# Two order changes in a two-layer fp32 kernel: what ScalarE and VectorE do around the first pair of each seven-product block, and a stacked layout for the long-convolution filters

## The reference, cut to what matters

```python
def swiglu_ffn(x, wi, wo):                  # d_model 1024, D_FF 2816, 512 tokens
    gate, up = jnp.split(x @ wi, 2, axis=-1)
    return (jax.nn.silu(gate) * up) @ wo

def hyena_filters(seqlen, w1, b1, w2, b2, w3, sin_freq):
    ...
    h = jnp.sin(sin_freq[0] * (zpos @ w1 + b1))
    h = jnp.sin(sin_freq[1] * (h @ w2 + b2))
    h = (h @ w3).astype(f32).reshape(seqlen, HY_ORDER, 2, HY_WIDTH)   # 512, 2, 2, 1024
    h = h * jnp.exp(-t * deltas)[:, None, None, :]
    return jnp.moveaxis(h, 0, 2)

def long_conv_bidir(u, h_fwd, h_bwd, bias):
    k = jnp.concatenate([h_fwd, jnp.zeros_like(h_fwd[:1]), h_bwd[:0:-1]], axis=0)
    ...                                     # product of spectra, inverse transform
```

## Time and profile before

| | |
|---|---|
| median of 3 runs | 4611.59 us (4609.36 to 4623.51) |
| profiled execution | 4627.68 us, its span 4625.9 us |
| PE busy | 4425.9 us (96%) |
| DVE busy | 3177.0 us (69%) |
| ACT busy | 1751.0 us (38%) |
| POOL busy | 2051.1 us (44%) |
| lines 2647 to 2649 (the seven products) on PE | 646.8 + 638.0 + 637.9 us |

### The profile page before, as it was taken

The page is one execution under the profiler, slowest core; times in us unless marked ns, Lnnn a source line. Parts: engine busy times, 40 slices in busy tenths (PEclk is TensorE's granted clock), DMA queues, the critical chain, the costliest instruction groups (busy, mean ns, idle before and its releaser), DMA issues.

```text
span 4625.9 us, 64527 instructions
## 1 busy us (share of the span) xinstructions
PE 4425.9 (96%) x25239; PEld 3828.8 (83%) x25239; DVE 3177.0 (69%) x4507; ACT 1751.0 (38%) x2753; POOL 2051.1 (44%) x1297
## 2 busy tenths in 40 slices
PE   7999999999999999999999999999999999998998
PEld 4757855779989999999899876798799878887997
DVE  4756667569869988788688355687488355555883
ACT  3334211233335543333345255444344243123442
POOL 2042024205887657788576100474276101124751
PEclk9999999999999999999999999899999999898999
DMA  4142411225776789999632321233232322001332
GB/s 174 52 145 96 145 62 54 91 87 172 258 240 218 256 330 391 375 384 385 235 96 92 100 75 46 73 101 96 78 99 94 96 85 73 24 33 59 97 101 73
DMA packets 229014, 664.15 MB, mean 144 GB/s; under 512 B 22039, under 2 KB 87975, under 8 KB 226536
## 3 DMA queue, kind: packets, MB, share of 16 engines
q1 hardware_dynamic: 112832, 398.26, 25.9%
q0 software_dynamic: 38752, 143.03, 8.4%
q10 hardware_dynamic: 77128, 118.73, 7.1%
HBM read 591.78 MB, written 68.16 MB: 143 GB/s over the span
## 4 chain that ended last, share of the span: by engine, by line
PE 63%; DVE 19%; POOL 7%; issue 5%; DMA 3%; ACT 3%; ACTq 0%; POOLq 0%; SPq 0%; DVEq 0%
PE ps L258 14%; PE ps L260 14%; PE ps L259 14%; DVE r L277 6%; POOL A L2882 3%; PE ps L1537 2%; DVE r L227 2%; POOL A L2823 2%; DVE A L1966 2%; PE ps L1616 1%; ACT r L274 1%; DVE A L2265 1%; PE ps L585 1%; DMA A<-in_f2i 1%; DMA A<-in_w_mod 1%
## 5 line engine op out<-in xcount | busy, mean ns | idle before, releaser
L258 PE MATMUL ps<-r,r 128*128 128x384 f32 (+2 forms) x3880 | 1427.2, 368 | 19.5 <-POOL r L227 11.6
L260 PE MATMUL ps<-r,r 128*128 128x384 f32 (+2 forms) x3880 | 1410.4, 363 | 0.0
L259 PE MATMUL ps<-r,r 128*128 128x384 f32 (+2 forms) x3880 | 1410.3, 363 | 0.0
L227 DVE TENSOR_TENSOR r<-A,r 128x1024 fp32r<-128x1024 f32 x428 | 585.5, 1368 | 718.0 <-ACT r L221 717.4
L221 ACT ACTIVATE r<-A 128x1024 fp32r<-128x1024 f32 x505 | 534.5, 1059 | 1246.4 <-PE ps L260 1046.9
L258 PEld LDWEIGHTS ps<-r,r 128*128 128x128 f32 x3880 | 733.2, 189 | 110.4 <-issue 20.4
L259 PEld LDWEIGHTS ps<-r,r 128*128 128x128 f32 x3880 | 732.9, 189 | 78.8 <-issue 3.4
L260 PEld LDWEIGHTS ps<-r,r 128*128 128x128 f32 x3880 | 732.2, 189 | 78.1
L277 DVE TENSOR_TENSOR r<-A,r 128x512 fp32r<-128x512 f32 x645 | 676.5, 1072 | 126.4 <-ACT r L274 122.6
L274 ACT ACTIVATE r<-A 128x512 fp32r<-128x512 f32 (+1 forms) x824 | 467.2, 607 | 712.3 <-POOL A L2882 431.8
L2647 PE MATMUL ps<-r,r 128*128 128x256 f32 x2240 | 646.8, 289 | 48.5 <-ACT A L2740 24.3
(11 more groups left out here) (526 smaller groups left out, 5839.4 us busy)
## 6 DMA issues: line engine op xcount, KB each, us to landing
A<-in_pu SPq DMA_DIRECT2D x128, 512.0 KB, 4.3
A<-in_pv SPq DMA_DIRECT2D x128, 512.0 KB, 6.8
A<-in_f1i SPq DMA_DIRECT2D x88, 512.0 KB, 3.5
A<-in_f2i SPq DMA_DIRECT2D x88, 512.0 KB, 3.5
A<-in_w_mod SPq DMA_DIRECT2D x48, 512.0 KB, 4.4
A<-in_w_in SPq DMA_DIRECT2D x48, 512.0 KB, 3.6
acts<-A ACTq DMA_DIRECT2D x128, 192.0 KB, 4.3
gates<-A ACTq DMA_DIRECT2D x8, 3072.0 KB, 11.4
```

Of the source, the lines that this page charges most:

```text
L227: e.tensor_tensor(self.vr(at + 1024, 1024), self.v(self.st0 + 1024 * (u % RS), 1024), self.vr(at, 1024).bitcast(F32), ALU.subtract).then_i ...
L258: t.matmul(o, hi, xh, start=first and k == k0, stop=False)
L259: t.matmul(o, hi, xl, start=False, stop=False)
L260: m = t.matmul(o, lo, xh, start=False, stop=final and k == K - 1)
```

## The change

Two things are changed.

In the blocks, the lists of ScalarE and VectorE are written in another order up to the start of pair 1. ScalarE now copies "one" of pair 0 directly behind the high part of operand 5, and makes the tokens' "22" high part and operands 6 to 10 behind it. VectorE makes the difference "22" only after operands 3, 4, 5 and `times_up` 1, and the table `EARLY_V` says which low parts stand behind which quarter sum for the first nine products. From the ninth product on both lists are as before.

In the filters, the second perceptron layer is made twice, on partitions 0 to 63 and 64 to 127 (its weights are loaded twice, side by side). The two 64-row weight slices are loaded to both partition halves too, the sum is made on the lower half and the difference on the upper half, and the two filters' products read different halves. The decay at tap 0 is halved on the host, and tap 0 is the sum of the two filters' first rows, copied to both, so the ninth product is gone.

```diff
@@ -1302,14 +1302,14 @@
         L.TB, L.KW, L.M, L.H2 = self.al(8192), self.al(2048), self.al(1536), self.al(512)
         L.DEC, L.W3 = self.HX, self.HX + 2048
         L.ZP, L.W12 = L.KW, L.KW + 1536
-        L.h, L.kk = self.A[0:64, L.KW + 1024:L.KW + 1536], self.A[0:64, L.KW + 512:L.KW + 1024]
-        L.hs = [self.A[0:64, L.H2:L.H2 + 512], self.A[0:64, L.W3 + 1536:L.W3 + 2048]]
-        L.a, L.b, L.sm = (self.A[0:64, L.W3 + 512 * i:L.W3 + 512 * i + 512] for i in range(3))
+        L.h, L.kk = self.v(L.KW + 1024, 512), self.v(L.KW + 512, 512)
+        L.hs = [self.v(L.H2, 512), self.v(L.W3 + 1536, 512)]
+        L.a, L.b, L.sm = (self.v(L.W3 + 512 * i, 512) for i in range(3))
 
         L.KWS, L.SQ = (L.OS, L.KW), L.OS + 2048
         L.ST = self.al(64)
 
-        fil, ks, us = (lambda r: [("fil", r, i) for i in range(9)]), (lambda r, f: [("ks", r, f, i) for i in range(4)]), (lambda r, f: [("us", r, f, i) for i in range(4)])
+        fil, ks, us = (lambda r: [("fil", r, i) for i in range(8)]), (lambda r, f: [("ks", r, f, i) for i in range(4)]), (lambda r, f: [("us", r, f, i) for i in range(4)])
         inv, tok = (lambda r: [("inv", r, c) for c in range(4)]), (lambda o: [("ut", o + i) for i in range(4)])
         self.plan([x for r in range(4) for x in us(r, 0) + us(r, 1) + inv(r)], range(4))
         self.plan([x for r in range(4) for x in fil(r) + (tok(4 * (r - 2)) if r in (2, 3) else []) + ks(r, 0) + ks(r, 1)], range(4, 8))
@@ -1320,8 +1320,8 @@
         L.parts = [(L.HF + 512 * k, L.TB + 512 * k) for k in range(8)]
         L.parts += [(L.UT + 512 * k, (L.OS if k < 4 else L.YF) + 512 * k) for k in range(8)]
 
-    def p64(self, name, k=0):
-        return self.A[0:64, self.prm0 + PRM[name][0] + k:self.prm0 + PRM[name][0] + k + 1]
+    def layer_rows(self, i):
+        return slice(0, 64) if i == 0 else slice(0, 128)
 
 
 
...
@@ -1332,16 +1332,17 @@
     def mlp_t(self, t, i):
         S, L = self.S, self.L2
         t.wait_ge(*S.at("hz") if i == 0 else S.at("layer", 0))
-        w, r = ((self.A[0:33, L.W12:L.W12 + 64], self.A[0:33, L.ZP:L.ZP + 512]), (self.A[0:64, L.W12 + 64:L.W12 + 128], L.h))[i]
-        t.matmul(self.PS[6][0:64, :], w, r, start=True, stop=True).then_inc(*S.on("t", "layer mm", i))
+        w, r = ((self.A[0:33, L.W12:L.W12 + 64], self.A[0:33, L.ZP:L.ZP + 512]), (self.A[0:64, L.W12 + 64:L.W12 + 192], L.h[0:64, :]))[i]
+        t.matmul(self.PS[6][self.layer_rows(i), :], w, r, start=True, stop=True).then_inc(*S.on("t", "layer mm", i))
 
     def mlp_v(self, v, i):
         S, L = self.S, self.L2
-        h, kk = L.h, L.kk
+        rows = self.layer_rows(i)
+        h, kk = L.h[rows, :], L.kk[rows, :]
         v.wait_ge(*S.at("layer mm", i))
-        v.tensor_scalar(h, self.PS[6][0:64, :], self.p64("hy_b1" if i == 0 else "hy_b2"), None, ALU.add).then_inc(*S.on("v"))
+        v.tensor_scalar(h, self.PS[6][rows, :], self.prm("hy_b1" if i == 0 else "hy_b2")[rows, :], None, ALU.add).then_inc(*S.on("v"))
         v.wait_ge(*S.last("v"))
-        v.tensor_scalar(h, h, self.p64("sinf", i), None, ALU.mult).then_inc(*S.on("v"))
+        v.tensor_scalar(h, h, self.prm("sinf", i)[rows, :], None, ALU.mult).then_inc(*S.on("v"))
         v.wait_ge(*S.last("v"))
         v.tensor_scalar(kk, h, float(1 / (2 * np.pi)), 12582912.0, ALU.mult, ALU.add).then_inc(*S.on("v"))
         v.wait_ge(*S.last("v"))
...
@@ -1461,7 +1462,8 @@
             a.wait_ge(*S.at("filter", r - 1))
         for i, x in enumerate((L.a, L.b)):
             at = 2048 * order + 1024 * i + 512 * half
-            a.dma_start(x, T["hy_w3"][:, at:at + 512]).then_inc(*S.dma("w3"))
+            for rows in (slice(0, 64), slice(64, 128)):
+                a.dma_start(x[rows, :], T["hy_w3"][:, at:at + 512]).then_inc(*S.dma("w3"))
         S.mark("w3", "w3", r)
         a.dma_start(self.v(L.DEC, 2048).rearrange("p (n c) -> p n c", n=4),
                     T["decay"][order].rearrange("(n p) c -> p n c", p=128)[:, :, 512 * half:512 * half + 512]).then_inc(*S.dma("dec", "filter decay", r))
@@ -1485,18 +1487,16 @@
             t.wait_ge(*S.at("u tokens", 0, 7))
             t.wait_ge(*S.at("hidden", 1))
         for nt in range(4):
-            for j, w in enumerate((L.sm, L.b)):
+            for j, rows in enumerate((slice(0, 64), slice(64, 128))):
                 ps = self.bank_t(t, "fil", r, 2 * nt + j)
-                t.matmul(ps[:, :], self.A[0:64, hh + 128 * nt:hh + 128 * nt + 128], w, start=True, stop=True).then_inc(*S.on("t", "fil", r, 2 * nt + j))
-        ps = self.bank_t(t, "fil", r, 8)
-        t.matmul(ps[0:1, :], self.A[0:64, hh:hh + 1], L.a, start=True, stop=True).then_inc(*S.on("t", "fil", r, 8))
+                t.matmul(ps[:, :], self.v(hh + 128 * nt, 128)[rows, :], L.sm[rows, :], start=True, stop=True).then_inc(*S.on("t", "fil", r, 2 * nt + j))
 
     def sums_v(self, v, r):
         S, L = self.S, self.L2
         v.wait_ge(*S.at("w3", r))
-        v.tensor_tensor(L.sm, L.a, L.b, ALU.add).then_inc(*S.on("v"))
-        v.wait_ge(*S.last("v"))
-        v.tensor_tensor(L.b, L.a, L.b, ALU.subtract).then_inc(*S.on("v", "filter sums", r))
+        for rows, how in ((slice(0, 64), ALU.add), (slice(64, 128), ALU.subtract)):
+            v.tensor_tensor(L.sm[rows, :], L.a[rows, :], L.b[rows, :], how).then_inc(*S.on("v"))
+        S.mark("v", "filter sums", r)
 
     def filters_v(self, v, r, ids):
         S, L = self.S, self.L2
@@ -1504,16 +1504,16 @@
         if r:
             v.wait_ge(*S.at("ks", r - 1, 1, 3))
         for i in ids:
-            v.wait_ge(*S.at("fil", r, i))
             nt, j = divmod(i, 2)
             if i < 8:
+                v.wait_ge(*S.at("fil", r, i))
                 v.tensor_tensor(self.v(L.HF + 2048 * j + 512 * nt, 512), self.ps("fil", r, i)[:, :], self.v(L.DEC + 512 * nt, 512), ALU.mult).then_inc(*S.on("v", "out", "fil", r, i))
                 continue
+            one, two = (self.A[0:1, L.HF + 2048 * j:L.HF + 2048 * j + 512] for j in range(2))
             v.wait_ge(*S.last("v"))
-            for j in range(2):
-                v.tensor_tensor(self.A[0:1, L.HF + 2048 * j:L.HF + 2048 * j + 512], self.ps("fil", r, 8)[0:1, :], self.A[0:1, L.DEC:L.DEC + 512], ALU.mult).then_inc(*S.on("v"))
-            S.mark("v", "out", "fil", r, 8)
-            S.mark("v", "filter", r)
+            v.tensor_tensor(one, one, two, ALU.add).then_inc(*S.on("v"))
+            v.wait_ge(*S.last("v"))
+            v.tensor_copy(two, one).then_inc(*S.on("v", "filter", r))
 
 
 
@@ -2710,6 +2710,7 @@
             a.wait_ge(*S.at("product", i, self.PAIRS - 1, {5: "s2", 9: "s1", 13: "s3", 17: "22"}[f]))
         self.part_hi(a, self.v(L.HID + 512 * f, 512), L.HI[f], 512, "hidden hi", i, f)
 
+    EARLY_V = {0: (), 1: (6,), 2: (7,), 3: (8,), 4: (9, 10), 5: (11, 12), 6: (13, 14), 7: (15, 16), 8: (17, 18)}
     LATE_A = {129: (0, 1), 130: (2, 3), 131: (4,), 134: (5,), 135: (6, 7), 136: (8, 9), 137: (10, 11), 138: (12,), 139: (13, 14)}
     LATE_V = {130: (0,), 131: (1,), 133: (3,), 134: (4,), 135: (6,), 136: (7,), 137: (9,), 138: (10,)}
 
@@ -2727,10 +2728,7 @@
                 self.token_a(a, i, "s3")
                 for n in range(1, 3):
                     self.operand_a(a, i, n)
-        for n in range(3, 7):
-            self.operand_a(a, i, n)
-        self.token_a(a, i, "22")
-        for n in range(7, 11):
+        for n in range(3, 6):
             self.operand_a(a, i, n)
         for m, (p, x) in enumerate(L.seven):
             if x == "11":
@@ -2740,6 +2738,10 @@
                 a.activation(self.v(L.CU + 512 * (p % 2), 256), self.ps("A", i, p)[:, 0:256], ACT.Copy).then_inc(*S.on("a", "one", i, p))
                 if p:
                     self.gate_half_a(a, i, p - 1, 1)
+                else:
+                    self.token_a(a, i, "22")
+                    for n in range(6, 11):
+                        self.operand_a(a, i, n)
             if x == "12":
                 self.gate_half_a(a, i, p, 0)
             self.operand_a(a, i, m + 11)
@@ -2839,18 +2841,18 @@
         self.operand_v(v, i, 1)
         self.token_lo_v(v, i, "s1")
         self.operand_v(v, i, 2)
-        self.token_v(v, i, "22")
         self.operand_v(v, i, 3)
         self.token_lo_v(v, i, "s3")
+        for n in range(4, 6):
+            self.operand_v(v, i, n)
         self.times_up_v(v, i, 1)
-        for n in range(4, 7):
-            self.operand_v(v, i, n)
-        self.token_lo_v(v, i, "22")
-        for n in range(7, 10):
-            self.operand_v(v, i, n)
+        self.token_v(v, i, "22")
         for m, (p, x) in enumerate(L.seven):
             self.quarter_v(v, i, p, x)
-            self.operand_v(v, i, m + 10)
+            if m == 1:
+                self.token_lo_v(v, i, "22")
+            for n in self.EARLY_V.get(m, (m + 10,)):
+                self.operand_v(v, i, n)
             for f in self.LATE_V.get(m, ()):
                 self.hidden_lo(v, "v", i, f)
             if m == 132:
@@ -4399,6 +4401,7 @@
```

(1 more changed line is left out.)

9 lines of the change are left out of this document (5 added, 4 removed).

## The result

| | before | after |
|---|---|---|
| median, 20 runs each on one chip | 4623.52 us | 4613.43 us |
| lowest and highest | 4609.36 to 4630.58 | 4604.66 to 4627.15 |
| ratio of the changed kernel to the one before | | 0.9982, 95% interval 0.9974 to 0.9991 |
| profiled execution | 4627.68 us | 4606.66 us |

By the ratio the change makes the kernel 8.3 us faster (4 to 12); the two medians lie 10.1 us apart. With 20 runs each, 8.3 us is told from none.

The account below looks back on a forecast made before the run. A loop of VectorE, GpSimd and ScalarE was taken to set the blocks' period, with TensorE waiting in it. Blocks 1.6 and filters 4.6 us off 4611.59 gave a median of 4605, range 4588 to 4616.

Parts of the forecast that it names:

- the filters' term: Filter rounds: overlap and the missing ninth product gain 2.2 + 1.4 + 1.0 = 4.6 us (3 to 7).
- The blocks' term: Four blocks: the new order of the lists gains 0.4 us a block, 1.6 in all.
- the limit of 0.3%: Whole kernel: a change of 0.3% (14 us) is about what this measurement tells from none.
- The stall moves, not goes.: Blocks: TensorE's 5.99 us wait at product 3 goes, and some 4.3 us of waiting appears at product 10.
- Operand 7 isn't earlier.: Blocks, VectorE: operand 7's low part stays 11.7 us behind product 0, within 0.7, so the raw load doesn't move.
- `gated` of pair 0 at 22.3, 0.5 us earlier.: Blocks: `gated` of pair 0 starts about 22.3 us behind product 0 (22.9 before), with the period of a pair unchanged.
- the first rival: Blocks: the 5.99 us wait and half clock go with nothing in their place, 4 times 10 us, 4565; chance 0.16.
- The clock at product 10: Blocks: after 4.3 us of idleness TensorE may run at 1.2 GHz from product 10, losing 4 us.
- The slower rival: Blocks: product 10 at half clock makes product 14 late, 10.4 us a launch lost, 4617 with the filters; chance 0.11.
- its sum of 5.9: Filters: the gain of about 5.9 us if the two row halves overlap as the skill states, without it 3.3.
- 4595 (VectorE faster up to operand 7): Blocks: the new order keeps GpSimd off the port, 2.9 us a block, 16 with the filters; chance 0.14.
- "Nothing": Filters and blocks: neither gives anything, 4609 to 4612; chance 0.07.

Follow-up runs that it names:

- e2: The kernel before with only the new order of the blocks' lists, filters as they were; ratio 1.0006 to before.
- e5: The changed kernel with four extra matmuls of constants on TensorE ahead of product 10 of each block; ratio 0.9981 to before.
- e4: The kernel before with ScalarE's order alone changed: "one" of pair 0, then the tokens' high part "22", directly behind operand 6; ratio 1.0006 to before.
- e8: The changed kernel with operand 7 made early, and "one" of pair 1 and the SiLU half ahead of operands 15 and 16; ratio 0.9976 to before.
- e7: The changed kernel with operand 7's high and low parts made ahead of the token difference "22"; ratio 0.9984 to before.
- e6: The changed kernel with ScalarE's "one" of pair 1 and SiLU half of pair 0 ahead of operands 15 and 16; ratio 1.0007 to before.
- e9: e6 with VectorE's quarter sums "one six" and "one five" of pair 1 ahead of the low parts of operands 15 to 18; ratio 0.9976 to before.
- e11: The changed kernel with only VectorE's quarter sums of pair 1 moved ahead of the low parts of operands 15 to 18; ratio 1.0004 to before.
- e10: e8 with VectorE's quarter sums of pair 1 ahead of the low parts of operands 15 to 18; ratio 0.9983 to before.
- e3: The kernel before with only the ninth filter product gone (halved decay at tap 0), filters not stacked on two halves; ratio 0.9986 to before.

## Why the prediction was right or wrong

The step that failed is the filters' term. It was put at 4.6 us and measured 8.2: the overlap of the two halves was counted half where it is full, VectorE's fourth copy-out of round 1 was held to stay where it was, and two transposes were moved ahead of the wait where four more go. The blocks' term was too large (1.6 against 0.9 or none). The mechanism of both terms is what the traces show; that 6.2 lies so near the measured 8.3 is in part luck, since the two errors pull in opposite directions. The second thing that failed is the limit of 0.3% below which a change was held not to be told from none: the interval of the ratio is 4 us to each side.

- **The stall moves, not goes.** Right. Product 10 was to start 22.1 us behind product 0 (35.35 against 13.28) and starts at 22.12; the idleness was put at 4.3 and is 4.18.
- **Operand 7 isn't earlier.** Right: forecast to end at 11.7 us behind product 0, it ends at 11.9. GpSimd's first sum again goes ahead only at VectorE's operation on PSUM: the sum starts at 1.15 us and takes 3.92, `times_up` starts at 3.84, and the VectorE operations that began in between, at 1.50, 2.64 and 3.24 us, kept their usual lengths (1.21, 0.67 and 0.68). That is the reading of the earlier trace rows and again not the order that the Trainium skill ("SBUF — State Buffer", "Who interferes with whom") gives; the price of that order, 0.8 us lost a block, didn't come.
- **`gated` of pair 0 at 22.3, 0.5 us earlier.** Nearly: 22.54 to 22.63, 0.2 to 0.5 us earlier than in the profile of before (mean 0.3). Blocks of other kernels with the old order reach 22.56 too, so even this isn't clear of scatter. The first period is 10.55 to 10.59 us (10.60 to 10.63 before), unchanged for this purpose.
- **0.4 us a block, 1.6 in all.** Measured 0.9 in the changed kernel and none in e2, which has the same lists. So a gain of the blocks is not shown; that it is far below the 40 us of the first rival is.
- **The clock at product 10** was to take some of the gain back. It does fall (0.51 of full speed for 4.9 us), for less than forecast: about 2.4 us of TensorE's time instead of 4. It costs nothing: e5 keeps it up and gains nothing. The slower rival's point of decision, product 14 ending over 1 us later than 31.8 us behind product 0, isn't reached: it starts at 30.05 and takes 1.44.
- **The filters, 4.6 us**: 8.2 in the changed kernel, 8.5 in the mean over the nine stacked kernels against the three old ones (243.2 against 251.6). Part of the means' difference can be the clock, at half for 34.1 to 41.0 us of this stretch in the stacked kernels and for 44.4 to 47.8 in the old ones; rounds 2 and 3 don't move with it. Round 0: 2.2 forecast, 3.3 in such means (14.6 to 11.4; 4.0 between the two profiled ones). I took the middle of "no overlap" and "full overlap"; the overlap is full. Of the first eight passes two each start 6 to 7 ns apart, and they take 1.99 instead of 3.70 us. "Filter" was forecast near 611.4 for full overlap, 11.6 us behind the first product, and comes at 11.4. Here the rule that stood beside the sum, the Trainium skill's "TensorEngine Tiling (Array Packing)", "Key Properties", was right, and its sum of 5.9 the nearer one. Round 1: 1.4 forecast, 2.3 measured in the means; the last products no longer wait for a copy-out that stands still but for one that comes 0.43 us earlier (7.48 against 7.91), and the half-clock discount of 0.4 didn't come. Rounds 2 and 3: 0.5 each forecast, 1.2 measured. There I moved two transposes ahead of the wait; with one bank use less it is four more, eight of sixteen instead of four, and 1.1 us.
- **Slips that changed little.** The first rival's 4565 is 4611.59 - 40 - 4.6 = 4567. Product 10 of before, at 2337.9, isn't "seven products of 1.44 behind the return of the clock" at 2331.7: it is 6.2 us, little over four products. The loads of round 1 didn't land over 10 us before the sums: VectorE stood 3.64 us for them before and stands 4.75 now. What covers this is that TensorE uses the sums over 15 us later.
- **The rivals.** 4565 (TensorE's stall is worth its length) fell with e2, e4 and e5. 4595 (VectorE faster up to operand 7) fell with the 11.9. "Nothing" fell with the interval and with the filters' times in the traces.

What is left open: whether the contention alone explains that e8, whose `gated` of pair 0 is 0.7 us earlier than e7's, gives no more than e7 (the rows fit, nothing tests it); and whether an order of VectorE's work exists that keeps the 2.2 us which e6 wins at `gated` of pair 0. The fastest by median is e8 (4609.40 us, ratio 0.9976, which e9 has too); its interval and the changed kernel's overlap, so only its blocks' time, 2.9 us less, says that it is better.

## What to carry to other kernels

A wait on the busiest engine is worth its length only if no loop of other engines sets the next meeting point; find that point (here `gated` of the first pair), measure its distance from the stage's start, and ask whether the edit moves it. Taking away an engine's first wait without looking at what stands behind it in the other engines' lists mostly moves the wait (e4, the change itself, e6), and one table row can turn a gain of 9 us into 2 by the stages' times (e11). Where two bounds are apart and a documented rule picks one end, weigh it by its own chance and not by the middle; here one such rule held (the overlap) and one didn't (the order of issue).

## What the runs showed of the hardware

**The scatter of one kernel has a place.** Between the end of the first block and the start of the second, code that no kernel here changes took 432.3 to 440.8 us by run. The stretch in e9 and in e10, which have the same code there (columns: length, busy us of PE, granted clock, DMA share, GB/s):

```profile
2525.63:2966.16 440.53, 425.93 (x1772) 0.96 0.23 71
```
```profile
2525.04:2957.51 432.47, 416.65 (x1772) 0.98 0.23 73
```

The clock was at half for 34.1 us of it in the four longest (before, e3, e4 and e9, 439.4 to 440.8) and for 13.7 in the three shortest (e8, e10 and e11, 432.3 to 432.5), and the other six lie between in both. Twenty us more at half clock would cost up to 10; the difference is 7 to 9. Before and after differ here by 6.1 us (439.36 against 433.24), and 3.9 more lie ahead of the first filter product (599.80 against 595.90; 595.9 to 601.1 over the thirteen kernels, whichever filters they have). So 10 of the 21 us between the two profiled executions are such scatter, 9 are the change's stages, and only times of single stages can be compared from one profile each.

**Contention goes by who has a pause.** Two low parts take 1.28 or 1.29 us alone, 2.35 to 2.71 where GpSimd works beside one of them or beside a part of both, and 3.12 to 3.43 beside a row of sums.
